# Pairing the halves of the TensorE array in the recurrence of a gated-linear-attention layer

## What is computed

```
b = cumsum(log_a)                                    # within the chunk
o_inter = (q * exp(b)) @ S                           # from the state before the chunk
att[i,j] = sum_d q[i,d] k[j,d] exp(b[i,d] - b[j,d])   # j <= i, "scores"
o = o_inter + att @ v                                # second term: the inner part
S = exp(b_last) * S + (k * exp(b_last - b)).T @ v    # "state product", 128 x 256
```

## Time and profile before

| what | value |
|---|---|
| median of 3 runs | 2007.36 us (2003.38 to 2016.0) |
| the profiled execution | 2010.96 us, its span 2009.3 us |
| mean granted PE clock | 0.916 |
| PE busy | 1893.0 us (94%), 13411 instructions |
| PEld, DVE, ACT, POOL busy | 84%, 44%, 23%, 4% |
| DMA | 218.72 MB, mean 109 GB/s |

### The profile page before, as it was taken

The page is one execution under the profiler, slowest core; times in us unless marked ns, Lnnn a source line. Parts: engine busy times, 40 slices in busy tenths (PEclk is TensorE's granted clock), DMA queues, the critical chain, the costliest instruction groups (busy, mean ns, idle before and its releaser), DMA issues.

```text
span 2009.3 us, 31177 instructions
## 1 busy us (share of the span) xinstructions
PE 1893.0 (94%) x13411; PEld 1693.8 (84%) x13411; DVE 892.4 (44%) x1652; ACT 470.5 (23%) x746; POOL 78.4 (4%) x146
## 2 busy tenths in 40 slices
PE   5989999999977899999999899999999899999998
PEld 3767778867746899999999787788879899999997
DVE  3433332254324563545453523265554754545452
ACT  1512221134443321111111332111123211111111
POOL 1000001400030000000000000000000000000000
PEclk7889999689897999999999999776759999999998
DMA  9567664500052212222223454120204222222211
GB/s 356 194 219 236 203 206 124 201 2 1 22 188 65 85 64 84 84 84 84 84 84 125 153 189 147 43 69 31 77 29 148 64 85 84 84 84 84 84 63 47
DMA packets 160173, 218.72 MB, mean 109 GB/s; under 512 B 7271, under 2 KB 131198, under 8 KB 159630
## 3 DMA queue, kind: packets, MB, share of 16 engines
q1 hardware_dynamic: 148814, 177.52, 26.7%
q0 software_dynamic: 11264, 39.86, 5.7%
HBM read 199.66 MB, written 21.76 MB: 110 GB/s over the span
## 4 chain that ended last, share of the span: by engine, by line
PE 90%; DVE 6%; ACT 2%; issue 1%; DMA 1%; SPq 0%; ACTq 0%; DVEq 0%
PE ps L1348 14%; PE ps L1346 13%; PE ps L1345 13%; PE ps L1034 4%; PE ps L1036 4%; PE ps L1035 4%; PE ps L1460 2%; PE ps L909 2%; PE ps L1136 2%; PE ps L1122 2%; PE ps L1311 2%; PE ps L1314 2%; PE ps L1312 2%; PE ps L960 1%; PE ps L1475 1%; PE ps L1078 1%
## 5 line engine op out<-in xcount | busy, mean ns | idle before, releaser
L1345 PE MATMUL ps<-arena_r,wring_r 128*128 128x288 f32 x2048 | 570.3, 293 | 7.4 <-DVE hbuf_r L2112 7.4
L1348 PE MATMUL ps<-arena_r,wring_r 128*128 128x288 f32 x2048 | 439.8, 296 | 0.0
L1345 PEld LDWEIGHTS ps<-arena_r,wring_r 128*128 128x128 f32 x2048 | 386.1, 189 | 7.7 <-issue 7.7
L1348 PEld LDWEIGHTS ps<-arena_r,wring_r 128*128 128x128 f32 x2048 | 328.7, 189 | 0.0
L1346 PE MATMUL ps<-hbuf_r,wring_r 128*128 128x288 f32 x1024 | 286.3, 295 | 0.0
L1346 PE MATMUL ps<-arena_r,wring_r 128*128 128x288 f32 x1024 | 284.5, 294 | 0.0
L1815 ACT ACTIVATE wring_r<-wring 128x2048 fp32r<-128x2048 f32 x64 | 122.5, 1917 | 618.5 <-DMA wring<-in_mlp_w 618.5
L1346 PEld LDWEIGHTS ps<-hbuf_r,wring_r 128*128 128x128 f32 x1024 | 193.9, 189 | 0.0
L1346 PEld LDWEIGHTS ps<-arena_r,wring_r 128*128 128x128 f32 x1024 | 192.4, 188 | 0.0
L2447 DVE SCALAR_TENSOR_TENSOR xbuf<-ps,mod,xbuf 128x288 f32<-128x288 f32 (+1 forms) x128 | 56.1, 480 | 245.5 <-PE ps L1348 245.5
L1034 PE MATMUL ps<-wring_r,xbuf_r 128*128 128x512 f32 x360 | 149.6, 415 | 0.0
(11 more groups left out here) (375 smaller groups left out, 2801.4 us busy)
## 6 DMA issues: line engine op xcount, KB each, us to landing
wring<-in_mlp_w SPq DMA_DIRECT2D x64, 1024.0 KB, 5.2
arena<-in_ada_w SPq DMA_DIRECT2D x40, 1024.0 KB, 5.8
wring<-in_even_w_in SPq DMA_DIRECT2D x14, 1024.0 KB, 7.8
wring<-in_gla_w_in SPq DMA_DIRECT2D x12, 1024.0 KB, 5.4
wring<-in_ada_w SPq DMA_DIRECT2D x4, 2048.0 KB, 28.0
xbuf<-xspill SPq DMA_DIRECT2D x2, 2304.0 KB, 8.8
arena<-in_cache_cmp_kv POOLq DMA_DIRECT2D x16, 256.0 KB, 10.1
wring<-in_cache_diff_k POOLq DMA_DIRECT2D x16, 256.0 KB, 3.1
```

The costliest lines, as they stand in the source:

```text
L1345: pe.matmul(bank, hi, x_hi[:, k, cols], start=k == 0, stop=False)
L1348: mm = pe.matmul(bank, lo, x_hi[:, k, cols], start=False, stop=k == KC - 1)
```

## The change

- Score matmuls are issued by turns for the even and the odd chunk of a pair, instead of one chunk after the other.
- The two state products of a pair go to two banks, 5 and 6 for even p, 1 and 2 (prompt) or 3 and 4 (samples) for odd p, and `st_first` is gone. Those of the samples are contracted over 32 rows each, w = 0 from rows 0 to 31 (samples 0 to 3), w = 1 from rows 32 to 63 (samples 4 to 7).
- Outputs are made by pairs of chunks: for each e both inner parts first (even chunk to bank 3, odd chunk to bank 4), then the two matmuls with the states. The pair waits once, for the state that its odd chunk reads: `s_ready >= NCH * h + 2 * k + 1`. The first pair has this wait too. The wait for the chunk before is gone.
- Since banks are shared in a new way, `g_prepare` and `g_samples` get a wait for `st_kept`, and the second to fourth product pair of the samples follow a wait for `go_kept`.
- ACT reads the outputs through a pattern that runs over both banks; DVE reads the new places.

```diff
--- before.py
+++ after.py
@@ -453,7 +453,6 @@
         att_mm = sem("att_mm")
         att_kept = sem("att_kept")
         st_mm = sem("st_mm")
-        st_first = sem("st_first")
         gkdm_ready = sem("gkdm_ready")
         st_kept = sem("st_kept")
         s_ready = sem("s_ready")
@@ -577,6 +576,13 @@
         gin_unit = [u // 2 if u < QK else 4 + 2 * ((u - QK) // (NT + 1)) for u in range(len(gin))]
         gin_used = [2 * n + 2 if n < 4 else QK + (NT + 1) * ((n - 4) // 2 + 1) for n in range(8)]
         R_FIRST = (0, 6, 11, 16)
+
+        def state_banks(p):
+            return (5, 6) if p % 2 == 0 else (1, 2) if p < 4 else (3, 4)
+
+        def state_sequence(p, w):
+            return p - 4 + 4 * w
+
 
         gin_order = ([("g", 0), ("u", 0), ("u", 1), ("z", 0), ("u", 2), ("z", 1), ("u", 3), ("z", 2), ("u", 4), ("z", 3)]
                      + [("u", u) for u in range(5, len(gin))])
@@ -1419,12 +1425,12 @@
                 if h:
                     pe.wait_ge(att_kept, h)
                     pe.wait_ge(kd_kept, h)
+                    pe.wait_ge(st_kept, 8 * h - 4)
                 for t in range(NT):
                     pe.transpose(ps[:, 1, t * P:(t + 1) * P], gkd[:, t * P:(t + 1) * P], ident[:, :])
                 pe.transpose(ps[0:TS, 0, 384:512], gkd[:, SEQ:T], ident[:, :]).then_inc(kd_turned, 1)
-                for c in range(NCH):
-                    lo = 64 * (c % 2)
-                    for i in range(4):
+                for c, i in [(2 * k + w, i) for k in range(NCH // 2) for i in range(4) for w in range(2)]:
+                        lo = 64 * (c % 2)
                         rhs = gqd[:, c, (i - 1) * SUB:i * SUB] if i else gqe[:, h % 2, c * GCH:c * GCH + SUB]
                         pe.matmul(ps[lo:lo + (i + 1) * SUB, 0, c // 2 * GCH + i * SUB:c // 2 * GCH + (i + 1) * SUB],
                                   gkp[i][:, c, :], rhs, start=True, stop=True)
@@ -1451,30 +1457,32 @@
                     pe.wait_ge(st_kept, x - 1)
                 for w in range(2):
                     if p < 4:
+                        rows = slice(64 * w, 64 * w + 64)
+                        lhs, rhs = gkdT[rows, h % 2, p, :], gv[rows, p, h * DVC:(h + 1) * DVC]
+                    else:
+                        rows = slice(32 * w, 32 * w + 32)
+                        lhs, rhs = gkdm[rows, state_sequence(p, w), :], gv[rows, NT, h * DVC:(h + 1) * DVC]
+                    mm = pe.matmul(ps[:, state_banks(p)[w], 0:DVC], lhs, rhs, start=True, stop=True)
+                mm.then_inc(st_mm, 1)
+
+            def g_outs(h, k):
+
+                pe.wait_ge(s_ready, NCH * h + 2 * k + 1)
+                for e in range(2):
+                    cols = slice(e * 4 * GCH + k * GCH, e * 4 * GCH + (k + 1) * GCH)
+                    for w in range(2):
                         lo = slice(64 * w, 64 * w + 64)
-                        lhs, rhs = gkdT[lo, h % 2, p, :], gv[lo, p, h * DVC:(h + 1) * DVC]
-                    else:
-                        lhs, rhs = gkdm[0:TS, 2 * (p - 4) + w, :], gv[0:TS, NT, h * DVC:(h + 1) * DVC]
-                    if p < 4 and w:
-                        pe.wait_ge(st_first, 4 * h + p + 1)
-                    mm = pe.matmul(ps[:, 5 + x % 2, w * DVC:(w + 1) * DVC], lhs, rhs, start=True, stop=True)
-                    if p < 4 and w == 0:
-                        mm.then_inc(st_first, 1)
-                mm.then_inc(st_mm, 1)
-
-            def g_out(h, c):
-
-                if c:
-                    pe.wait_ge(s_ready, NCH * h + c)
-                    pe.wait_ge(go_mm, NCH * h + c)
-                lo = slice(64 * (c % 2), 64 * (c % 2) + 64)
-                for e in range(2):
-                    o = ps[:, 3 + e, c * GCH:(c + 1) * GCH]
-                    if c:
-                        pe.matmul(o, sp_[:, c % 4, e * P:(e + 1) * P], gqe[:, h % 2, c * GCH:(c + 1) * GCH], start=True, stop=False)
-                    mm = pe.matmul(o, gv[lo, c // 2, h * DVC + e * P:h * DVC + (e + 1) * P], gatt[lo, h % 2, c // 2, :],
-                                   start=c == 0, stop=True)
-                mm.then_inc(go_mm, 1)
+                        mm = pe.matmul(ps[:, 3 + w, cols], gv[lo, k, h * DVC + e * P:h * DVC + (e + 1) * P], gatt[lo, h % 2, k, :],
+                                       start=True, stop=k == 0 and w == 0)
+                        if e and k == 0 and w == 0:
+                            mm.then_inc(go_mm, 1)
+                    for w in range(2):
+                        c = 2 * k + w
+                        if c:
+                            mm = pe.matmul(ps[:, 3 + w, cols], sp_[:, c % 4, e * P:(e + 1) * P], gqe[:, h % 2, c * GCH:(c + 1) * GCH],
+                                           start=False, stop=True)
+                            if e:
+                                mm.then_inc(go_mm, 1)
 
             def g_prompt(h):
                 pe.wait_ge(att_kept, h + 1)
@@ -1483,30 +1491,27 @@
                     pe.wait_ge(go_kept, h)
                 g_states(h, 0)
                 g_states(h, 1)
-                g_out(h, 0)
+                g_outs(h, 0)
                 last = R_FIRST[min(h + 1, HC - 1)]
                 if 0 < h < HC - 1:
                     for i in range(R_FIRST[h], last - 3):
                         r_half(i)
                 g_states(h, 2)
-                g_out(h, 1)
-                g_out(h, 2)
+                g_outs(h, 1)
                 g_states(h, 3)
-                g_out(h, 3)
                 if h == 0:
                     for i in range(last - 3):
                         r_half(i)
                 if h + 1 < HC:
                     r_half(last - 3)
-                g_out(h, 4)
-                g_out(h, 5)
+                g_outs(h, 2)
                 if h + 1 < HC:
                     r_half(last - 2)
-                g_out(h, 6)
-                g_out(h, 7)
+                g_outs(h, 3)
 
             def g_samples(h):
                 pe.wait_ge(s0_loaded[h % 2], 16 * (h // 2 + 1))
+                pe.wait_ge(st_kept, 8 * h + 4)
                 for e in range(2):
                     o = ps[:, 2, e * TS:(e + 1) * TS]
                     pe.matmul(o, gv[0:TS, NT, h * DVC + e * P:h * DVC + (e + 1) * P], gatt[0:TS, h % 2, 4, :], start=True, stop=True)
@@ -1515,7 +1520,9 @@
                                        gqe[:, h % 2, SEQ + DS * n:SEQ + DS * n + DS], start=False, stop=True, skip_group_check=True)
                 mm.then_inc(os_mm, 1)
                 pe.wait_ge(gkdm_ready, h + 1)
-                for p in range(4, 8):
+                g_states(h, 4)
+                pe.wait_ge(go_kept, h + 1)
+                for p in range(5, 8):
                     g_states(h, p)
 
             g_prepare(0)
@@ -1902,7 +1909,8 @@
             def g_keep_prompt(h):
                 act.wait_ge(go_mm, NCH * (h + 1))
                 for e in range(2):
-                    act.activation(go[:, e, h, 0:SEQ], ps[:, 3 + e, :], ACT.Copy)
+                    act.activation(go[:, e, h, 0:SEQ].rearrange("p (k w t) -> p w k t", k=NCH // 2, w=2),
+                                   ps[:, 3:5, e * 4 * GCH:(e + 1) * 4 * GCH].rearrange("p w (k t) -> p w k t", k=NCH // 2), ACT.Copy)
 
             def g_keep_samples(h):
                 act.wait_ge(os_mm, h + 1)
@@ -2564,7 +2572,7 @@
                     dve.wait_ge(st_mm, 8 * h + p + 1)
                     for w in range(2):
                         c = 2 * p + w
-                        kv = ps[:, 5 + (8 * h + p) % 2, w * DVC:(w + 1) * DVC]
+                        kv = ps[:, state_banks(p)[w], 0:DVC]
                         if NCH * h + c + 1 >= 4:
                             last = NCH * h + c + 1 - 4
                             dve.wait_ge(go_mm, last + 1)
@@ -2593,9 +2601,9 @@
                 for p in range(4, 8):
                     dve.wait_ge(st_mm, 8 * h + p + 1)
                     for w in range(2):
-                        n = 2 * (p - 4) + w
+                        n = state_sequence(p, w)
                         ins = dve.scalar_tensor_tensor(out=s0[:, h % 2, n, :], in0=s0[:, h % 2, n, :], scalar=gebl[:, h % 2, NCH + n:NCH + n + 1],
-                                                       in1=ps[:, 5 + (8 * h + p) % 2, w * DVC:(w + 1) * DVC], op0=ALU.mult, op1=ALU.add)
+                                                       in1=ps[:, state_banks(p)[w], 0:DVC], op0=ALU.mult, op1=ALU.add)
                     ins.then_inc(st_kept, 1)
 
             def r_gate(i):
```

## The result

The changed kernel takes **1958.62 us** (median of 4 runs, 1958.14 to 1965.22); the kernel before, on the same chip, 2007.05 (4 runs, 2003.38 to 2016.0). The ratio is 0.9763, with a 95% interval of 0.9727 to 0.9798.

A forecast was written before the change was run, and what follows sets the result against it. PE was taken as the bound (90% of the chain of waits), full of small matmuls at a low clock. Terms -10 - 5.4 - 2.0 + 0.2 - 0.8 - 12.0 = -30 gave 1977 us beside the median, range 1960 to 2000.

The forecast's parts named there:

- the r_halves, left at nothing: R_halves in the stage: no gain in the sum; heads 1 and 2 carried 9.0 us for two r_halves.
- Scores, -10: Score matmuls of four heads, 20.66 us: even and odd chunks overlap, saving 10 us, with bounds 0 and 10.3.
- The feed rival: Scores: PE gets them no faster per instruction than now, 81 ns, so nothing of the 10 is saved; 1987 us, chance 0.06.
- Head 0's stretch, 10.4: Head 0, products and outputs of chunks 0 to 3: 15.83 us become 10.4, saving 5.4.
- Sample products, 5.2 from ACT's copy to DVE's last read: Sample products: 32-row pairs overlap fully and DVE's reads are the bound; 8.0 us become 5.2, saving 2.8 and 2.1.
- The rival without overlap: 32-row products and scores: pairs don't overlap where the trace doesn't show it; saving only 12, 1995 us, chance 0.15.
- The new wait: Heads 1 and 2, outputs 0 and 1 wait for the state after chunk 0: loss 8.1 and 6.4 us.
- up to 14 more: Sign of error: if PE's gaps before the first outputs of heads 1 and 2 are absent, up to 14 us faster.
- Third product to the next r_half at the high clock, 3.5: Heads 1 and 2, third product, outputs 2 and 3, fourth product: 9.38 and 8.70 us become 3.5, saving 5.9 and 5.2.
- The rival in which PE stays at 1.2 GHz behind the stall: Heads 1 and 2: after idling, PE stays at 1.2 GHz up to the next head; saving only 12, 1995 us, chance 0.12.
- Head 3, 36.9 with DVE late: Head 3, ACT's copy to DVE's last read: 48.9 us become 36.9 with DVE late, saving 12.0.
- Slower: Whole kernel: the new wait outweighs the rest, with stalls of about 21 us; 2017 to 2027 us, chance 0.09.

## Why the prediction was right and wrong

- **The step that failed: the r_halves, left at nothing** ("clock in heads 1 and 2 better or worse by 3 each" was all the range held for them). They gained 12.5 us: 3.0 in head 0, 5.6 and 3.9 in heads 1 and 2. The sum carried over what they took before ("two r_halves 9.0") as if it were theirs. Most of the gain, 9.4 us at 5, 8, 10, 13 and 15, had been the price of serial work ahead: with the scores serial again 5, 10 and 15 are slow again, with the outputs serial again 5, 8, 13 and 15 (and 4, which was not slow before). The 1.5 us that r_half 9 gained were lost again in neither run. The clock was taken up as a rival in one direction only. What in the work of PE makes the clock fall stays open beyond this.
- **Scores, -10:** measured -12.1. The overlap was sized well at the clock of before; the higher clock came on top. With the r_halves this is 14.6 of the 18.5 us missing. The other 3.9 are spread over the heads (1.1 and 2.3 more saved in heads 0 and 2, 1.2 less in head 1, 1.7 more in head 3); they were not traced one by one. The feed rival (81 ns a matmul) is out: 34 ns. The 31 ns of the earlier trace rows were read as a feed without changes; the loop behind that line goes round four quarters of the array's columns (`ps[32 * q:32 * q + 32]`), so it showed the overlap itself (serial ones of only 16 columns take 66 at that clock).
- **Head 0's stretch, 10.4:** measured 9.97.
- **Sample products, 5.2 from ACT's copy to DVE's last read:** measured 5.16; 32-row pairs overlap in full (two pairs in 2.08, the same as two 64-row pairs at 1268.41 in head 0). The rival without overlap is out; undoing it cost 12.9.
- **The new wait:** third product 28.7 and 26.0 after ACT's copy: measured 28.3 (1341.53 less 1313.27) and 25.4; gaps of "some 10 and 8": 10.63 and 7.87. Taking them away gave 13.2 and 16.6, "up to 14 more" had been said.
- **Third product to the next r_half at the high clock, 3.5:** measured 3.0 in head 1. The rival in which PE stays at 1.2 GHz behind the stall is out: r_half 6 is slow (4.61, 4.96 before), r_half 7 already takes 3.18.
- **Head 3, 36.9 with DVE late:** measured 35.3 (1417.19 to DVE's last read, 1452.45), with DVE late and PE waiting 1.59 for the third sample product.
- **Slower:** it was to decide where less than 15 us were saved outside the stalls; 48.5 were saved with the stalls in.

## What to carry to other kernels

When PE alternates between small and dense matmuls, price the dense ones too: compare one dense block behind sparse work with the same block behind dense work, and count the difference as a term of whatever makes the sparse work shorter or denser. A term that hangs on the clock needs a bound on the side of gain as well as of loss. When a wait is moved ahead of work, look for what the engine that signals does just before: reordering DVE's list was worth another 16.6 us of the stage here, and touched nothing on PE.

## What the chip showed beyond this

- Matmuls in different parts of the array overlap: in two halves of its rows (two products in 1.23 us at 1.2 GHz, one alone in 1.22), in two 32-row quarters (four products in 2.08), and in two halves of its columns, with 16 to 64 columns each (34 ns each, against 66 when serial at the same clock: 4.20/64).
- PE listed as busy for a whole stretch says nothing of its clock: 5.99 of 5.99 us busy, at 0.52, in the kernel before.
- With a stall of 10.63 us behind it, an r_half took 4.61 us and the next 3.18, so it was back at the high level; without the stall (DVE's list reordered) the first took 4.20. Taking away 18.5 us of stalls in two heads gave 16.6: a stall cost no more than its own length.
